# Prompt attention: values between the two turnings, next logits last, first keys in four pieces

## The reference

```python
def sb_block(q_blk, q_start, k, v, bias):
    # A[t,s] = sigmoid(z_ts) * prod_{s<j<t} (1 - sigmoid(z_tj)), strictly causal
    valid = k_pos[None, :] < q_pos[:, None]
    z = jnp.einsum('bqhd,bkhd->bhqk', q_blk, k) + bias[None, :, None, None]
    lneg = jnp.where(valid, jax.nn.log_sigmoid(-z), 0.0)
    suffix = lax.cumsum(lneg, axis=3, reverse=True) - lneg
    w = jnp.where(valid, jnp.exp(jax.nn.log_sigmoid(z) + suffix), 0.0)
    return jnp.einsum('bhqk,bkhd->bqhd', w, v)
```

## Time and profile before

| | |
|---|---|
| median of 3 runs | 3711.01 us (3707.94 to 3712.34) |
| the profiled execution | 3709.46 us, span 3707.9 us |
| TensorE busy | 3375.2 us, 91% of the span |
| VectorE busy | 1654.0 us, 45% |
| ScalarE busy | 1433.5 us, 39% |
| GpSimd busy | 760.3 us, 21% |
| mean granted TensorE clock | 0.953 |
| the prompt attention | from about 2020 to 3113 us of the span |

### The profile page before, as it was taken

One profiled execution on the slowest core, in us unless ns is written; L12 is line 12 of the kernel. 1 busy time (PEld: TensorE's weight loads), 2 busy tenths in 40 slices (PEclk: granted clock), 3 DMA queues, 4 the chain that ended last, 5 costly groups with the idle time before them and its releaser, 6 DMA issues. The chain is left out here.

```text
span 3707.9 us, 50217 instructions
## 1 busy us (share of the span) xinstructions
PE 3375.2 (91%) x17844; PEld 2411.1 (65%) x17844; DVE 1654.0 (45%) x1964; ACT 1433.5 (39%) x2341; POOL 760.3 (21%) x807
## 2 busy tenths in 40 slices
PE   7999997877689799999997999999999997888798
PEld 6999996444378699999997444444444443444487
DVE  4111111777633321111110688888888885333333
ACT  5111112666422211111111677777777773333321
POOL 0000000000001000000000566666666763000000
PEclk9999998888899899999998799999999998999999
DMA  4222212233245432222212513223232202999843
GB/s 138 69 69 72 76 58 97 88 113 106 92 177 170 149 103 69 69 69 69 69 66 90 163 52 103 80 57 91 80 99 55 63 18 90 401 364 363 331 140 108
DMA packets 240437, 439.20 MB, mean 118 GB/s; under 512 B 26005, under 2 KB 149722, under 8 KB 227962
## 3 DMA queue, kind: packets, MB, share of 16 engines
q1 hardware_dynamic: 225130, 351.88, 28.5%
q0 software_dynamic: 15152, 85.34, 6.4%
HBM read 313.03 MB, written 124.13 MB: 118 GB/s over the span
## 5 line engine op out<-in xcount | busy, mean ns | idle before, releaser
L1582 POOL TENSOR_TENSOR att_w<-att_w,att_rest 128x1023 f32<-128x1023 f32 (+7 forms) x384 | 614.0, 1601 | 330.0 <-DVE att_rest L1542 246.4
L1423 PEld LDWEIGHTS att_wT_acc<-const_ident,att_w 128*128 128x128 f32 x2176 | 231.2, 141 | 410.7 <-issue 254.5
L416 PE MATMUL projb_acc<-projb_x_hi,projb_w_hi 128*128 128x416 f32 x1280 | 452.4, 353 | 26.3 <-DVE projb_x_lo L407 26.3
L416 PE MATMUL projb_acc<-projb_x_hi,projb_w_lo 128*128 128x416 f32 x1280 | 450.0, 352 | 0.0
L416 PE MATMUL projb_acc<-projb_x_lo,projb_w_hi 128*128 128x416 f32 x1280 | 449.7, 351 | 0.0
L1453 PE MATMUL att_z<-att_k,att_q 64*128 64x512 f32 (+3 forms) x1280 | 403.6, 590 | 2.5 <-ACT att_w L1504 2.4
L1542 DVE TENSOR_TENSOR_SCAN att_rest<-att_rest,att_zero 128x128 f32<-128x128 f32 (+7 forms) x256 | 359.9, 1408 | 73.3 <-ACT att_rest L1496 71.9
L1423 PE MATMUL att_wT_acc<-const_ident,att_w 128*128 128x128 f32 x2176 | 375.1, 289 | 5.9 <-ACT att_k_tok L1511 2.7
L1496 ACT ACTIVATE att_rest<-att_z,att_bias 128x1024 f32<-128x1024 f32 (+7 forms) x384 | 333.3, 868 | 88.3 <-PE att_z L1453 86.9
L274 PE MATMUL proja_acc<-proja_x_hi,proja_w_hi 128*128 128x416 f32 x1000 | 353.4, 353 | 0.8 <-DVE proja_x_lo L247 0.7
L274 PE MATMUL proja_acc<-proja_x_hi,proja_w_lo 128*128 128x416 f32 x1000 | 351.5, 352 | 0.0
(11 more groups left out here) (224 smaller groups left out, 4670.7 us busy)
## 6 DMA issues: line engine op xcount, KB each, us to landing
smp_k_pages<-in_cache_k SPq DMA_DIRECT2D x128, 512.0 KB, 8.8
smp_v_pages<-in_cache_v SPq DMA_DIRECT2D x128, 512.0 KB, 9.8
proj_b<-projb_out POOLq DMA_DIRECT2D x32, 1040.0 KB, 4.6
proj_a<-proja_out POOLq DMA_DIRECT2D x24, 1040.0 KB, 4.5
att_q<-proj_b SPq DMA_DIRECT2D x128, 128.0 KB, 2.9
att_k<-proj_b SPq DMA_DIRECT2D x32, 512.0 KB, 9.5
proja_w_raw<-in_w_in_a SPq DMA_DIRECT2D x24, 512.0 KB, 4.1
gla_vgT<-proj_a SPq DMA_DIRECT2D x24, 512.0 KB, 5.7
```

The costliest lines, as they stand in the source:

```text
L416: mm = pe.matmul(acc[:, q, 0:size], w[:, b, k, :], x[:, k, at:at + size], start=(k == 0 and w is w_hi and x is x_hi), stop=(k == KD - 1 an ...
L1423: mm = pe.transpose(wT_ps[:, h, (t % 4) * P:(t % 4 + 1) * P], weight(pair, phase, h, t, at, P), c.ident[:, :])
L1582: pool.tensor_tensor(these, these, passed[:, 1:size], ALU.mult).then_inc(w_made, 1)
```

## The change

TensorE issues, for a value item, the turning of head 0, then the product with the values of the item before, then the turning of head 1, and then the next logits. Before, the logits stood between the two turnings and the product came last. Query and key loads take both heads in one transfer (two transfers of twice the size in place of four). The keys of pair 0 are loaded in four pieces of 512 tokens, each with its own semaphore; pieces 1 and 3 are issued behind the raw keys and values. The waits of `logits` follow from that.

```diff
+        in_first_k = s.sems("in_first_k", NCH)
...
             def load_k(pair):
-                for h in range(2):
-                    row = k_rows + pair * P + h * HD
-                    for half in range(2):
-                        sp.dma_start(k2[half * HD:(half + 1) * HD, pair % 2, h, :], projT[row:row + HD, 0:SEQ]
-                                     ).then_inc(in_k[pair % 2], 16)
+                row = k_rows + pair * P
+                for half in range(2):
+                    sp.dma_start(k2[half * HD:(half + 1) * HD, pair % 2, :, :],
+                                 projT[row:row + P, 0:SEQ].rearrange("(h p) n -> p h n", p=HD)
+                                 ).then_inc(in_k[pair % 2], 16)
...
             def load_q(pair, g):
-                for h in range(2):
-                    row = q_rows + pair * P + h * HD
-                    for half in range(2):
-                        sp.dma_start(q2[half * HD:(half + 1) * HD, g, h, :],
-                                     projT[row:row + HD, g * BANK:(g + 1) * BANK]).then_inc(in_q[g], 16)
+                row = q_rows + pair * P
+                for half in range(2):
+                    sp.dma_start(q2[half * HD:(half + 1) * HD, g, :, :],
+                                 projT[row:row + P, g * BANK:(g + 1) * BANK].rearrange("(h p) n -> p h n", p=HD)
+                                 ).then_inc(in_q[g], 16)
...
+            def load_first_k(u):
+                for half in range(2):
+                    sp.dma_start(k2[half * HD:(half + 1) * HD, 0, :, u * BANK:(u + 1) * BANK],
+                                 projT[k_rows:k_rows + P, u * BANK:(u + 1) * BANK].rearrange("(h p) n -> p h n", p=HD)
+                                 ).then_inc(in_first_k[u], 16)
+
             load_q(0, 0)
-            load_k(0)
+            load_first_k(0)
             sp.dma_start(bias[:, 0, :], b_sb.unsqueeze(0).broadcast_to([P, NH])).then_inc(bias_in, 16)
             load_q(0, 2)
+            load_first_k(2)
             load_raw(0)
+            load_first_k(1)
+            load_first_k(3)
             load_gate(0)
...
             def logits(n):
                 _, pair, phase, t, h, lo, hi, carried = z_items[n]
-                pe.wait_ge(in_k[pair % 2], 64 * (pair // 2 + 1))
-                pe.wait_ge(in_q[t // 4], 64 * (pair + 1))
+                if pair == 0:
+                    for u in range(lo // BANK, -(-hi // BANK)):
+                        pe.wait_ge(in_first_k[u], 32)
+                elif pair % 2:
+                    pe.wait_ge(in_k[1], 32 * (pair // 2 + 1))
+                else:
+                    pe.wait_ge(in_k[0], 32 * (pair // 2))
+                pe.wait_ge(in_q[t // 4], 32 * (pair + 1))
...
                 elif kind == "a":
                     turn_weights(0, pair, *x)
+                    if behind:
+                        multiply_values(*behind)
+                    behind = (pair, *x)
+                    turn_weights(1, pair, *x)
                     if order[i - 1][0] == "z" and made < len(z_items):
                         logits(made)
                         made += 1
-                    turn_weights(1, pair, *x)
-                    if behind:
-                        multiply_values(*behind)
-                    behind = (pair, *x)
```

## The result

The changed kernel takes 3793.61 us in the median of 4 runs (3789.25 to 3797.87), the kernel before 3710.37 (4 runs): a ratio of 1.0225, with a 95% interval of 1.0207 to 1.0242. It is slower by 83 us. Predicted were 3797 and a range of 3765 to 3822.

The account below looks back on a forecast made before the run. TensorE set the pace before; after, a two-beat round trip through TensorE, ScalarE and VectorE would. 80 + 9 + 5 - 6.7 = 87 us on 3709.5 or the median 3711 gave 3797, range 3765 to 3822.

Parts of the forecast that it names:

- The loop v, T1, z, pass, scan, copy, v of two beats: Prompt attention: values product (v), head 1 turning (T1), logits (z), ScalarE pass, VectorE scan and copy; 7.11 us per two beats.
- 89, 5 and -6.7: Prompt attention stage, in us: loss in the pairs (80 and 9), loss in the tail, gain from the loads; sum 87.
- One pair: Single-logit beats 8 to 39 of a head pair, walked in stretches: 11.4 us longer per pair.
- The last term: End of a pair's walk: the first values product after it still waits 0.7 us for its copy.
- 80 and 9: Loss in us: 80 over seven pairs; 9 in pair 0, where waiting for raw keys and values absorbs the first 2.2.
- The tail: Beats after the last logits: the values product waits for the copy, 2.54 us instead of 2.03; ten times 0.5, +5.
- The loads: Start of the stage: fewer bytes ahead of the logits; first logits 8 us earlier, gain 6.7 us, bounds 4 and 8.5.
- The row of 258 GB/s: Profile row at the stage's start, taken as 2 KB query rows; grounds for expecting no loss from smaller key pieces.
- Copy in time: Rival in the attention beats: VectorE's copy comes in time, TensorE stays the pace, only loads act; 3704 us, chance 0.08.
- A shorter loop: Rival in the attention beats: the four handoffs overlap by 0.3 us in all; 3772 us, chance 0.17.
- The clock: Rival in the attention stage: pockets of idle TensorE bring its clock down, 50 us on top; 3847 us, chance 0.03.
- Some 25 waits a pair: Sign in the timeline: TensorE's values product waits for VectorE's copy some 25 times a pair, 0.2 to 0.9 us each.

Follow-up runs that it names:

- the loads alone: The kernel before with only the new loads (both heads per transfer, first keys in four pieces), TensorE's order as before; 3706.15 us, ratio 0.9985.
- after_copy_first: The changed kernel with VectorE's copy of head 1 ahead of the scan of the same beat; 3804.49 us, ratio 1.0257.

## Why the prediction was right, point by point

- **The mechanism.** The loop v, T1, z, pass, scan, copy, v of two beats was shown from both sides: the scan taken out of it (by order, or by size) brings 75 us back, a fill of 0.27 us put into it makes one turn 0.23 us longer and leaves the full beats of the old order as they were, and moving only the logits ahead of the values removes it. Its length, 7.11 predicted, is 7.10. The sum holds term by term: 89, 5 and -6.7 were predicted, 86.1, 5.0 and -8.4 are measured in the stage.
- **One pair.** 11.4 us predicted; 10.5 measured (141.95 to 142.12 against 131.5). By stretches, T0 of beat 8 to 13 takes 18.53 us, as walked; 13 to 19 22.1 for 22.3; 19 to 24 17.2 for 17.2; 24 to 31 22.0 for 22.3; 31 to 40 31.1 for 30.8. The last term failed: the 0.7 us of the first v of the next pair is 0.1, since TensorE is that late itself. It was counted twice.
- **Six, not seven times.** From the store in pair 0's turn beats to that of pair 6, 65.9 us are lost: 62.8 by six periods and 3.1 more, 2.7 of them in one pair in which the clock fell; from there to the last logits 19.3, for the rest of pair 6 and pair 7, whose beats have no turning of keys and values beside them (a reading of the schedule, not tested). With 0.9 up to the first of these, against the loads alone, where waits for the raw keys and values absorbed the loss as foreseen, it is 86 for the 89 of the sum (80 and 9).
- **The tail.** 5.0 for 5. Its beats:

```profile
3170.50 1.08 PE L1447 MATMUL att_o_acc<-att_wT,att_v_tok 128*64 128x512 f32 x4 [0.44 <-DVE att_wT L1575]
...
3173.04 1.08 PE L1447 MATMUL att_o_acc<-att_wT,att_v_tok 128*64 128x512 f32 x4 [0.44 <-DVE att_wT L1575]
```

  2.54 apart, as worked out.
- **The loads.** 6.7 predicted, within 4 to 8.5; the loads alone take 8.4 off the stage, 5.9 of it at the third logits and the rest in pair 0. Counted from SP's first issue, the first logits came 7.3 sooner instead of 8; they stand at 2030.0 and not near 2027, since that issue was 2.1 later in the profiled execution. The row of 258 GB/s was read as one of query rows of 2 KB alone; half of its bytes were already key rows of 8 KB (38 of 249 packets between 2023 and 2025.6, 0.31 of 0.65 MB). Pieces of 2 KB rows moved at 213 and 227 GB/s, whole rows of 8 KB at 204 to 238 in the kernel before: the figure by size that the Trainium skill gives ("DMA: Bandwidth & Descriptors", section "Bandwidth"), by which the start would gain 5 instead of 8, was not what happened. It is a figure for a transfer of 64 KB, and the pieces here are 256 KB each and queued one behind the other, so it was the wrong row to take.
- **The rivals.** Copy in time: no. A shorter loop: no. The clock was half right, and my row against it was read badly. The earlier trace rows has the clock at 1.00 in a stretch with little work, but it fell at the end of that very stretch:

```profile
2086.00:2088.00 2.00, 1.39 (x7) 1.35 (x7) 0.24 (x1) 0.46 (x1) 0.00 (x0) 0.52 0.00 0
```

  In the changed kernel it fell once in the six middle pairs, behind the waits of a group's first products:

```profile
2518.00:2522.00 4.00, 2.98 (x19) 1.46 (x19) 4.00 (x4) 3.11 (x5) 2.06 (x2) 0.97 0.36 95
2522.00:2528.00 6.00, 6.00 (x22) 3.12 (x21) 2.74 (x4) 2.46 (x4) 3.04 (x4) 0.50 0.21 69
```

  That pair took 144.65 us, 2.7 more. The other pairs had such waits too and kept the full clock, so what made the difference in this one stays open; with idle pockets of 2 us (`after_copy_first`) it fell in each of six stretches of a pair's length (means 0.95 to 0.98). The rule of the Trainium skill ("TensorE: Matmul & The Clock Gate", section "HAM oscillation — how this bites in real kernels"), that waits in a loop bring it down again and again, agrees with that experiment (mean clock of the run 0.939 against 0.955) and less with the change itself, whose waits are 0.2 to 1.1 us and where it fell once.
- **What it would show.** "Some 25 waits a pair" was wrong: 97 in some six pairs, about 16 a pair, because of the interleaving; for the same reason full beats are not 3.5 to 3.6 us apart but 3.24 and 3.86 in turn. The pairs of 145 us were 134 plus the loss, and the 134 was no period, as said above.

## What to carry to other kernels

When work is moved on one engine, count how many beats lie between a result and the instruction that depends on it through all engines: a reordering that leaves an engine's own work unchanged can shorten that from three beats to two and make the round trip the pace. What stands in line ahead of the awaited instruction on the other engine is part of the path; moving it is as good as making it faster, but then the next in line is to be checked (the gate here, the copy of the keys in the turn beats). Try transposes next to transposes on TensorE where the dependencies allow it; for other kinds of blocks nothing here shows a gain.

## What the runs showed that was not expected

Two groups of four transposes cost 1.02 us side by side and 1.17 apart, although no instruction waits for another engine in either place. Why is open. I had written that the four blocks have the same cost in any order because each has a turning beside it; the tail of the kernel before already had the 1.02. Logits ahead of values are 1.06 apart, the same as ahead of a turning. The order T0, logits, values, T1 with the new loads is the fastest kernel of this study, 0.64% under the kernel before. It was not tried with a tail of its own, where the old order is 0.5 us a beat faster.

At the start of the stage the granted clock stayed at its lower level for long, in both kernels: 0.50 up to about 2072 us before and 2064 after, although TensorE was busy 10.00 of 10 us from 2040 to 2050 and again from 2050 to 2060. Why it rose no sooner is open.
